# Openings of three weight units, a shorter norm chain behind the post-norms and a reordered beginning in an fp32 two-block network on one core

## The chip, the core and the metric

One core of a Trainium2 chip runs the whole program in one launch. The metric is the device time of that launch in microseconds; three runs of a kernel give its median. A profile is taken of one further execution.

## The reference

Two layers in a row on an activation of 512 positions by 1024 channels, all in fp32. Cut to what matters here:

```python
def first_block(x, ...):   # x: (1, 512, 1024)
    z = split(rmsnorm(x, norm_mix_pre) @ w_in)            # 25 column blocks of 128
    y = concat(rwkv7(z0), mlstm(z1), swa(z2), fox(z3)) @ w_out
    x = x + rmsnorm(y, norm_mix_post)
    u, g = rmsnorm(x, norm_ffn_pre) @ ffn_w_up            # 2 x 22 column blocks
    y = (u * gelu(causal_dwconv(g))) @ ffn_w_down
    return x + rmsnorm(y, norm_ffn_post)

def second_block(x, ...):
    x = x + 0.5 * swiglu(rmsnorm(x, ffn1_norm), w_gate, w_up, w_down)
    x = x + hybrid_mixer(rmsnorm(x, mix_norm), w_in, ..., w_out)
    x = x + 0.5 * swiglu(rmsnorm(x, ffn2_norm), w_gate, w_up, w_down)
    return rmsnorm(x, final_norm)
```

rmsnorm divides each position by the root of the mean square over its 1024 channels and multiplies by a gain per channel.

## The kernel before, in words

**Layout.** Activations are kept transposed: eight tiles xt[0..7] of 128 channels by 512 positions. A projection is a row of products "128x128 weight block times 128x512 tile", summed over the blocks in one PSUM bank.

**Precision by splitting.** TensorE runs in fp32r, a shorter format. Every fp32 operand is split in a head (the value rounded to fp32r) and a tail (what is left), and a block costs three products: head x head, head x tail, tail x head. For an activation tile, head(k, gain) is an ACT copy into hH[k] (with the gain as scale) and tail(k, gain, a) a DVE instruction into hL[k]. The factor of the norm, rB, is not multiplied into the tiles but into the result of the projection. So a projection behind a pre-norm can begin before rB is known; only what reads its result waits.

**Weights.** The class Stream brings them. A unit is one output column block of 128 with up to eight weight blocks of 128x128 (512 KB). SP's queue loads units in their order into two raw buffers (RAW = 2) and waits, before it loads a unit, until the unit two places before it has been split. A piece is half a unit: four blocks, 128x512. split(i) puts an ACT copy (the head) into ACT's queue and a subtraction (the tail) into DVE's; in mixer 1's projections every second subtraction goes to POOL. There are six buffers for split pieces (CUT = 6). ahead(n) (L246) issues the splits of all pieces up to n beyond the one now in use. Each split waits until its buffer has been used, which one semaphore, s_used, counts.

Every engine works through its queue in the order in which build() writes the instructions down. Inside the mixers a planner (drive_by, L400; drive, L387) chooses by estimated costs which chain writes next, with the projections as filler; elsewhere the order is that of the text.

- product / parts (L267, L314): one projection of one or three units. At the start of every piece it calls ahead(CUT - 1), thus five pieces ahead; then come four times three products.
- pair / pair_steps (L276, L285): two units side by side, block by block, so that for each tile k six products follow as soon as its head and tail are there. Used at the start of every projection behind a pre-norm, and for the first two units of mixer 1's output projection. It calls ahead(CUT - 1) at its start and its end.

**Norms.** square_in(k, ...) (L1603) has ACT square tile k and adds it to one of two sums: even k on POOL into acc, odd k on DVE into acc2. finish_norm (L1619) loads the Ln table by a small activation, sums over the channels by two fp32 products with a matrix of ones, and takes Ln and Exp (rstd_of) of the result, which gives rB. pre_norm (L1632) issues heads and tails that are not yet made, then ahead(CUT), then squares that are not yet made, and leaves finish_norm to be called later, as p.rms. A post-norm lies behind a down or output projection: project_out and ffn square each of the eight results as it comes and keep it in y[n] with its gain; add_post (L1719) then finishes the norm, multiplies y[n] by rB on DVE, adds it to xt[n] (DVE for n = 0 and 4, POOL for the others) and issues head and tail of each tile.

**Stages.** 1: mixer 1, whose output projection has a post-norm. 2: FFN 1 with a convolution, Gelu and a post-norm. 3: FFN 2 (gate, Silu, up, down) without post-norm. 4: mixer 2, no post-norm. 5: FFN 3. 6: the final norm. In an FFN the loop over f = 0..21 makes a gate and an up product each; the text behind them for that f stands ahead of the products for f + 1: multiply by rB (DVE), activation (ACT), product of both (POOL), head copy (ACT), tail (POOL). For f = 0 the products are a pair; then comes the gate product of f = 1 in bank 2 ("early"), then p.rms(). In the mixers the class Begun (L345) does this: pair, first half of a third unit, p.rms(), and the other half when its result is asked for.

**The beginning** (L1575 to L1600, L1781). ACT's queue loads two small constant arrays, pk (gains and the like) and cA (identity, ones), SP's the first weight unit, then all eight x tiles, then the second unit. All four engines wait until both constant arrays have come. Then come the splits of the first unit, heads and tails of all tiles, further splits and the squares.

## Time and profile before

| what | us |
|---|---|
| median of 3 runs | 1740.0 (1739.81 to 1741.82) |
| the profiled execution, its own time | 1741.66 |
| its span, first to last instruction | 1739.8 |
| TensorE busy | 1654.2 |
| VectorE busy | 820.3 |
| ScalarE busy | 697.7 |
| GpSimd busy | 289.2 |
| mean granted TensorE clock, as a share of full speed | 0.981 |

In the rows, PE is TensorE's products, PEld its weight loads, DVE VectorE, ACT ScalarE, POOL GpSimd, SP SyncE. "t" is any SBUF tile, "bank" a PSUM bank. A row of the timeline gives start, length, engine, line, operation, output<-input with shapes, and how many instructions were merged; in brackets, how long the engine had been idle before it and what ended that. An fp32 product (those with ones) stands as two instructions. L198 is the helper that most products come from, L304 the products of a pair, L335 the last product of a piece, L257 the ACT half and L261 the DVE or POOL half of a weight split, L158 and L165 other activations, L170, L180 and L176 DVE and POOL arithmetic.

### The profile page before, as it was taken

What the parts mean: (1) busy time and instruction counts of PE and PEld (TensorE: products, weight loads), DVE (VectorE), ACT (ScalarE), POOL (GpSimd) and SP (SyncE); (2) the same over time, 40 slices, a digit from 0 to 9 for tenths busy, and PEclk for the clock granted to TensorE, in tenths of its full rate; (3) what the DMA queues carried; (4) which work ended last, traced back from release to release, by engine and by line L of the source; (5) the groups of instructions that cost most, each with busy time, mean ns of one, the idle gap of its engine ahead of it and who ended that gap; (6) DMA issues with size and microseconds to landing.
All of it is one profiled execution on the core that took longest, in us unless ns stands there. A gap on an engine that the chain in (4) does not pass through costs nothing.

```text
span 1739.8 us, 21730 instructions
## 1 busy us (share of the span) xinstructions
PE 1654.2 (95%) x8578; PEld 1338.9 (77%) x8578; DVE 820.3 (47%) x1276; ACT 697.7 (40%) x1255; POOL 289.2 (17%) x241
## 2 busy tenths in 40 slices
PE   6999998988999999979999999999999999999995
PEld 5776776667888888858888888878887788888884
DVE  4566344355655542255444433367455444444332
ACT  5556445545433333245333332244533433333222
POOL 1221110023222210022222210000010122222001
PEclk9999998989999999999999999999999999999998
DMA  4220011121332233313222323322132232232331
GB/s 166 85 74 26 14 49 37 58 100 61 110 97 97 97 93 98 100 49 109 97 97 97 97 88 101 103 80 86 37 101 83 72 112 96 99 97 93 98 100 58
DMA packets 44133, 148.37 MB, mean 85 GB/s; under 512 B 5064, under 2 KB 6144, under 8 KB 44032
## 3 DMA queue, kind: packets, MB, share of 16 engines
q1 hardware_dynamic: 40032, 140.53, 24.9%
q10 hardware_dynamic: 4000, 6.46, 1.1%
q8 instruction: 68, 1.11, 0.3%
q14 instruction: 33, 0.27, 0.0%
HBM read 144.86 MB, written 2.10 MB: 84 GB/s over the span
## 4 chain that ended last, share of the span: by engine, by line
PE 87%; DVE 6%; ACT 5%; issue 1%; POOL 1%; DMA 0%; DVEq 0%; ACTq 0%; POOLq 0%
PE bank L198 76%; PE bank L335 6%; PE bank L304 3%; DVE t L170 3%; ACT t L158 2%; DVE t L180 2%; ACT L158 1%; PE bank L206 1%; DVE t L261 1%; ACT t L257 1%; POOL t L170 1%; DVE t L184 0%; DMA t<-in_cst 0%; DVE t L190 0%; ACT t L165 0%
## 5 line engine op out<-in xcount | busy, mean ns | idle before, releaser
L198 PE MATMUL bank<-t 128*128 128x512 f32 (+6 forms) x7578 | 1516.3, 360 | 26.8 <-DVE t L170 10.0
L198 PEld LDWEIGHTS bank<-t 128*128 128x128 f32 (+3 forms) x7578 | 1161.1, 179 | 296.8 <-issue 36.8
L261 DVE TENSOR_TENSOR t<-t 128x512 fp32r<-128x512 f32 (+1 forms) x516 | 394.3, 795 | 436.4 <-ACT t L257 428.8
L170 POOL TENSOR_TENSOR t<-t 128x512 f32<-128x512 f32 (+1 forms) x181 | 239.4, 1322 | 1210.0 <-DVE t L170 563.3
L257 ACT ACTIVATE t<-t 128x512 fp32r<-128x512 f32 (+1 forms) x540 | 310.7, 613 | 261.2 <-PE bank L335 216.9
L158 ACT ACTIVATE t<-t 128x512 f32<-128x512 f32 (+6 forms) x351 | 202.6, 605 | 357.7 <-DVE t L170 169.6
L170 DVE TENSOR_TENSOR t<-bank,t 128x512 f32<-128x512 f32 (+4 forms) x238 | 147.4, 630 | 237.2 <-PE bank L335 213.7
L335 PE MATMUL bank<-t 128*128 128x512 f32 x516 | 200.7, 389 | 0.0
L165 ACT ACTIVATE t<-t 128x512 fp32r<-128x512 f32 (+3 forms) x87 | 51.7, 606 | 250.0 <-POOL t L170 247.6
L170 DVE TENSOR_TENSOR t<-t 128x512 f32<-128x512 f32 (+7 forms) x135 | 96.6, 733 | 72.2 <-ACT t L158 62.0
L180 DVE SCALAR_TENSOR_TENSOR t<-t 128x512 f32<-128x512 f32 (+3 forms) x142 | 104.0, 748 | 39.7 <-ACT t L158 38.3
L304 PE MATMUL bank<-t 128*128 128x512 f32 x288 | 80.1, 438 | 40.8 <-DVE t L180 34.6
L335 PEld LDWEIGHTS bank<-t 128*128 128x128 f32 x516 | 96.9, 188 | 20.3
L304 PEld LDWEIGHTS bank<-t 128*128 128x128 f32 x288 | 60.3, 214 | 59.2 <-issue 34.1
L180 DVE SCALAR_TENSOR_TENSOR t<-bank,t 128x512 f32<-128x512 f32 (+5 forms) x60 | 33.1, 568 | 83.6 <-PE bank L335 60.9
L165 ACT ACTIVATE t<-bank 128x128 f32<-128x128 f32 (+5 forms) x106 | 38.2, 389 | 74.9 <-PE bank L198 47.6
L158 ACT ACT_TABLE_LOAD x50 | 64.2, 1283 | 0.9
L261 POOL TENSOR_TENSOR t<-t 128x512 fp32r<-128x512 f32 x24 | 33.6, 1401 | 148.9 <-ACT t L257 135.6
L158 ACT ACTIVATE t<-bank,t 128x512 f32<-128x512 f32 (+5 forms) x68 | 39.1, 578 | 22.1 <-PE bank L198 11.0
L158 ACT ACTIVATE t<-bank 128x512 f32<-128x512 f32 x20 | 12.0, 599 | 59.3 <-PE bank L335 38.9
L206 PE MATMUL bank<-t 128*128 128x128 f32 x196 | 30.4, 285 | 1.4 <-DVE t L170 1.3
L206 PEld LDWEIGHTS bank<-t 128*128 128x128 f32 x196 | 21.5, 142 | 7.1 <-issue 2.1
(22 smaller groups left out, 90.0 us busy)
## 6 DMA issues: line engine op xcount, KB each, us to landing
t<-in_ffn_w_up SPq DMA_DIRECT2D x88, 512.0 KB, 4.4
t<-in_w_in SPq DMA_DIRECT2D x50, 512.0 KB, 3.5
t<-in_ffn_w_down SPq DMA_DIRECT2D x48, 512.0 KB, 3.5
t<-in_ffn_w_gate SPq DMA_DIRECT2D x44, 512.0 KB, 3.4
t<-in_ffn_w_down SPq DMA_DIRECT2D x24, 384.0 KB, 3.1
t<-in_w_out SPq DMA_DIRECT2D x16, 512.0 KB, 3.5
t<-in_xt SPq DMA_DIRECT2D x8, 256.0 KB, 5.9
t<-in_xt ACTq DMA_DIRECT2D x8, 256.0 KB, 4.6
```

The costliest lines, as they stand in the source:

```text
L158: return self.av.do(lambda e: e.activation(out, in_, func, bias=bias, scale=scale, **({} if accum is None else {"accum_out": accum})), *de ...
L165: return q.do(lambda e: e.activation(out, in_, ACT.Copy), *deps, us=us)
L170: return q.do(lambda e: e.tensor_tensor(out, a, b, op), *deps, us=self.cost(out, q, True))
L180: return self.dv.do(lambda e: e.scalar_tensor_tensor(out=out, in0=a, scalar=s, in1=b, op0=op0, op1=op1), *deps, us=self.cost(out, self.dv, ...
L198: fn = lambda e: e.matmul(out, w, x, start=start, stop=stop, skip_group_check=True)
L206: fn = lambda e: e.transpose(out, in_, ident)
L257: self.p.av.put(lambda e: e.activation(hi, raw, ACT.Copy), self.s_head, 1, (self.s_load[u % RAW], 16 * (u // RAW + 1)), (self.s_used, i - ...
L261: q.put(lambda e: e.tensor_tensor(lo, raw, hi.bitcast(F), SUB), self.s_tail[i % 2], 1, (self.s_head, i + 1), before, us=0.79 if q is self. ...
L304: fn = lambda e, o=outs[u], w=w, x=x, a=(k == 0 and n == 0), z=(k == 7 and n == 2): e.matmul(o, w, x, start=a, stop=z, skip_group_check=True)
L335: pe.put(lambda e, lo=lo, x=x, stop=stop: e.matmul(out, lo, x, start=False, stop=stop, skip_group_check=True), self.s_used, 1, us=0.227)
```

## The change

- Stream has a semaphore for each of its six piece buffers in place of the one count s_used.
- pair is gone; open takes two or three units. It calls ahead(2 x units) at its start. First come, for every tile k, the products that need only the tile's head (weight head x head and weight tail x head, of all units), then, for every k, those with the tile's tail. It waits for heads (p.heads), not for tails, in its first half. It has no call of ahead at its end. pair_steps stays for mixer 1's output projection.
- FFNs open with three units (f = 0's gate and up, f = 1's gate), and p.rms() comes right behind. Begun does the same in mixer 2; in mixer 1 (late=True) it opens with two, then makes the third unit as a plain product, then calls p.rms().
- Post-norms: the Ln table is loaded ahead of the projection; sums, the two ones products over results 0 to 6, are written into product 7 (behind its first piece in an output projection, its third in a down projection); rest squares result 7 and adds it by a ones product of its own, followed by seven ones products of 384 columns whose result nobody reads, a call of ahead(CUT - 1), Ln and Exp. y[7] is made on DVE.
- add_post: all additions on DVE, all heads as they come, a call of ahead(CUT) behind tile 1, and the eight tails behind all of it. square_in takes own=True to add on DVE: for result 6 and for pre_norm's squares.
- The beginning: pk and cA have counters of their own; DVE, ACT and POOL wait for pk only, and all for cA behind the first pre_norm. x tile 0 is loaded between weight units 0 and 1, tiles 1 to 7 between units 1 and 2. acc is set to zero and three products of zeros run on TensorE. ACT's first table load comes without a wait for a transfer. The order on ACT is then split 0, head 0, splits 1 and 2, heads 1 and 2, split 3, heads 3 to 7.

The diff, cut to its core:

```diff
+        self.s_used = [sem(f"s_used{n}") for n in range(CUT)]
...
-            if u == 1:
-                others(sp)
+            if u > 0:
+                others(sp, u)
...
+    def used(self, i):
+        return (self.s_used[i % CUT], i // CUT + 1)
...
+    def open(self, outs, xh, heads, xl, *free):
+        pe, at = self.p.pe, self.at
+        part = lambda t, u, k: t[(at + 2 * u + k // 4) % CUT][:, (k % 4) * 128:(k % 4) * 128 + 128]
+        self.ahead(2 * len(outs))
+        for k in range(8):
+            for u, out in enumerate(outs):
+                i = at + 2 * u + k // 4
+                self.p.mm(out, part(self.hi, u, k), xh[k], k == 0, False, heads[k], (self.s_head, i + 1), *free)
+            for u, out in enumerate(outs):
+                self.p.mm(out, part(self.lo, u, k), xh[k], False, False, self.tail(at + 2 * u + k // 4))
+        for k in range(8):
+            for u, out in enumerate(outs):
+                fn = lambda e, o=out, w=part(self.hi, u, k), x=xl[k][0], z=k == 7: e.matmul(
+                    o, w, x, start=False, stop=z, skip_group_check=True)
+                if k % 4 == 3:
+                    pe.put(fn, self.used(at + 2 * u + k // 4)[0], 1, xl[k][1], us=0.227)
+                else:
+                    pe.quiet(fn, xl[k][1], us=0.227)
+        self.at += 2 * len(outs)
+        return [self.used(at + 2 * u + 1) for u in range(len(outs))]
...
     def product(self, W, banks, xh, xl):
         if self.rms:
-            two = [banks.next(), banks.next()]
-            m = W.pair([b.t[:, :] for b in two], xh, xl, *[b.free for b in two])
-            self.done = list(zip(two, m))
-            yield
-            self.third = W.parts(self.extra.t[:, :], 1, xh, xl, self.extra.free)
-            next(self.third)
+            three = [banks.next(), banks.next(), self.extra]
+            opened = three[:2] if self.late else three
+            m = W.open([b.t[:, :] for b in opened], xh, W.p.heads, xl, *[b.free for b in three])
+            if self.late:
+                m.append(W.product(self.extra.t[:, :], 1, xh, xl))
+            self.done = list(zip(three, m))
             self.rms()
             self.rms = None
+            yield
...
-        def load_x(sp):
-            for k in range(8):
+        def load_x(sp, u):
+            for k in {1: range(1), 2: range(1, 8)}.get(u, ()):
...
-        for q in (p.dv, p.av, p.po, p.pe):
-            q.wait(have)
+        blank = p.mset(acc[:, :], 0.0, q=p.dv)
...
+        for _ in range(3):
+            idle = p.mm(bank[6].t[:, :], acc[:, 0:128], acc[:, :], True, True, blank, last=True)
+        for q in (p.dv, p.av, p.po):
+            q.wait(named)
...
+        def sums(b):
+            p.mm(b.t[:, :], ones, acc[:, :], True, False, state["acc"], b.free)
+            state["acc_read"] = p.mm(b.t[:, :], ones, acc2[:, :], False, False, state["acc2"], last=True)
+
+        def rest(b, src, *deps):
+
+            a = p.act(sq[1][:, :], src, ACT.Square, state["sq"][1], *deps)
+            state["sq"][1] = m = p.mm(b.t[:, :], ones, sq[1][:, :], False, True, a, last=True)
+            for _ in range(7):
+                p.mm(bank[7].t[:, 0:CA], ones, cA[:, :], True, True, bank[7].free)
+            W.ahead(CUT - 1)
+            b.free, state["rB"] = rstd_of(b.t[:, :], 1.0 / 1024, eps[:, 0:1], rB[:, :], m, state.get("rB_read"))
+            return a
...
                     if f == 0:
-                        mg, mu = W.pair([bg.t[:, :], bu.t[:, :]], xh, xl, bg.free, bu.free)
-                        early = W.product(bank[2].t[:, :], 1, xh, xl, bank[2].free)
+                        three = [bg, bu, bank[2]]
+                        mg, mu, early = W.open([b.t[:, :] for b in three], xh, p.heads, xl, *[b.free for b in three])
                         p.rms()
...
+        def add_post(then, y, yt):
+
             for n in range(8):
                 a = p.tt(y[n][:, :], y[n][:, :], rB[:, :], MUL, yt[n], state["rB"])
-                xtok[n] = p.tt(xt[n][:, :], xt[n][:, :], y[n][:, :], ADD, a, xtok[n], q=p.dv if n % 4 == 0 else p.po)
-                heads.append(head(n, then))
-                if n:
-                    made[n - 1] = tail(n - 1, then, heads[n - 1])
-            made[7] = tail(7, then, heads[7])
+                xtok[n] = p.tt(xt[n][:, :], xt[n][:, :], y[n][:, :], ADD, a, xtok[n])
+                begun[n] = head(n, then)
+                if n == 1:
+                    W.ahead(CUT)
+            for n in range(8):
+                made[n] = tail(n, then, begun[n])
...
-        W.ahead(2)
+        W.ahead(1)
         if 1 in stages:
+            for k in range(8):
+                begun[k] = head(k, "norm_mix_pre")
+                if k in (0, 2):
+                    W.ahead(3 if k == 0 else 4)
+            for k in range(8):
+                made[k] = tail(k, "norm_mix_pre", begun[k])
             xh, xl = pre_norm("norm_mix_pre", bank[7])
```

## Rows read from the trace of the kernel before

**Rows 1.** The page: engines' busy time; the costliest group of PSUM reads on DVE.

```profile
PE 1654.2 (95%) x8578; PEld 1338.9 (77%) x8578; DVE 820.3 (47%) x1276; ACT 697.7 (40%) x1255; POOL 289.2 (17%) x241
...
L170 DVE TENSOR_TENSOR t<-bank,t 128x512 f32<-128x512 f32 (+4 forms) x238 | 147.4, 630 | 237.2 <-PE bank L335 213.7
```

**Rows 2.** Timeline of the boundary FFN 1 to FFN 2.

```profile
752.40 0.39 PE L335 MATMUL bank<-t 128*128 128x512 f32 x1
...
752.89 0.60 ACT L158 ACTIVATE t<-bank 128x512 f32<-128x512 f32 x1 [3.51 <-PE bank L335]
...
754.27 1.12 PE L198 MATMUL bank<-t 128*128 128x512 f32 x2 [0.61 <-DVE t L170]
...
755.12 1.28 ACT L158 ACT_TABLE_LOAD   x1
...
759.16 2.02 DVE L170 TENSOR_TENSOR t<-t 128x512 f32<-128x512 f32 x3 [3.25 <-ACT t L158]
...
763.28 4.49 PE L304 MATMUL bank<-t 128*128 128x512 f32 x12 [7.89 <-DVE t L180]
...
785.91 4.42 PE L198 MATMUL bank<-t 128*128 128x512 f32 x15
```

**Rows 3.** Stretch behind that wait: length, engines' busy time, granted clock, DMA.

```profile
763.20:766.00 2.80, 2.72 (x7) 2.19 (x8) 2.80 (x3) 0.58 (x2) 1.65 (x1) 0.50 0.00 0
```

**Rows 4.** Timeline of FFN 2: the norm's Ln, the next weight split.

```profile
787.96 0.67 ACT L158 ACTIVATE t<-bank,t 128x512 f32<-128x512 f32 x1
...
794.54 1.14 ACT L257 ACTIVATE t<-t 128x512 fp32r<-128x512 f32 x2
...
795.19 2.03 DVE L261 TENSOR_TENSOR t<-t 128x512 fp32r<-128x512 f32 x2 [3.22 <-ACT t L257]
```

**Rows 5.** The same in FFN 1, with convolution and Gelu.

```profile
407.03 0.69 ACT L158 ACTIVATE t<-bank,t 128x512 f32<-128x512 f32 x1 [0.18 <-PE bank L198]
...
416.21 2.05 DVE L261 TENSOR_TENSOR t<-t 128x512 fp32r<-128x512 f32 x2 [2.74 <-ACT t L257]
```

**Rows 6.** Timeline of the entry into mixer 2.

```profile
1130.39 11.04 PE L304 MATMUL bank<-t 128*128 128x512 f32 x48
...
1132.46 1.14 ACT L257 ACTIVATE t<-t 128x512 fp32r<-128x512 f32 x2
...
1149.48 2.78 PE L198 MATMUL bank<-t 128*128 128x512 f32 x11 [0.84 <-DVE t L170]
```

**Rows 7.** Timeline of the entry into FFN 3.

```profile
1354.13 0.39 PE L335 MATMUL bank<-t 128*128 128x512 f32 x1
...
1355.28 5.53 ACT L158 ACTIVATE t<-t 128x512 f32<-128x512 f32 x9 [3.70 <-DVE t L170]
...
1356.56 5.39 DVE L180 SCALAR_TENSOR_TENSOR t<-t 128x512 fp32r<-128x512 f32 x8
...
1357.45 12.56 PE L304 MATMUL bank<-t 128*128 128x512 f32 x48 [2.94 <-DVE t L180]
1360.72 1.14 ACT L257 ACTIVATE t<-t 128x512 fp32r<-128x512 f32 x2
...
1375.29 4.42 PE L198 MATMUL bank<-t 128*128 128x512 f32 x15
```

**Rows 8.** Timeline of the beginning.

```profile
6.07 0.25 POOL L195 MEMSET t<- 128x1 f32 x2 [5.62 <-DMA t<-in_cst]
...
8.74 4.99 ACT L158 ACTIVATE t<-t 128x512 fp32r<-128x512 f32 x8
...
15.67 12.03 PE L304 MATMUL bank<-t 128*128 128x512 f32 x45 [3.53 <-DVE t L261]
...
35.73 2.78 PE L198 MATMUL bank<-t 128*128 128x512 f32 x11 [0.83 <-DVE t L170]
```

**Rows 9.** The page's DMA issues: number, KB each, median us to landing.

```profile
t<-in_xt SPq DMA_DIRECT2D x8, 256.0 KB, 5.9
```

**Rows 10.** Timeline of the boundary mixer 1 to FFN 1, inside the opening.

```profile
393.86 5.98 PE L304 MATMUL bank<-t 128*128 128x512 f32 x18 [1.86 <-DVE t L180]
```

More of the change, by code:

```diff
@@ L1 @@
+import itertools
 import math
@@ L298, in pair_steps @@
                 ops = [(hi, xh[k]), (hi, xl(k)[0]), (lo, xh[k])]
-                signal = 1 if (k == 3 and u == 0) or (k == 7 and u == 0) else 2 if k == 7 else 0
                 pe.wait(self.tail(i), *free)
@@ L305, in pair_steps @@
                         o, w, x, start=a, stop=z, skip_group_check=True)
-                    if n >= 3 - signal:
-                        pe.put(fn, self.s_used, 1, xl(k)[1], us=0.227)
+                    if n == 2 and k % 4 == 3:
+                        pe.put(fn, self.used(i)[0], 1, us=0.227)
                     else:
@@ L533, in run @@
         pb = Banks([bank[0], bank[1]])
-        begun = Begun(p.rms, bank[3])
+        begun = Begun(p.rms, bank[3], late=True)
         end, tok, used = {}, {}, {}
@@ L1636, in pre_norm @@
             for k in range(8):
-                if made[k] is None:
-                    made[k] = tail(k, gain, head(k, gain))
+                if begun[k] is None:
+                    begun[k] = head(k, gain)
+                    made[k] = tail(k, gain, begun[k])
             W.ahead(CUT)
@@ L1699, in ffn @@
                 yt = []
+                if post:
+                    log_table()
                 for n in range(8):
                     b = bank[4 + n % 2]
-                    m = W.product(b.t[:, :], 3, [t[:, :] for t in fH],
-                                  [(fL[i][:, :], fl[i]) for i in range(22)], b.free)
-                    if post:
-                        square_in(n, b.t[:, :], m)
+                    g = W.parts(b.t[:, :], 3, [t[:, :] for t in fH],
+                                [(fL[i][:, :], fl[i]) for i in range(22)], b.free)
+                    m = ended(g, 3, (lambda: sums(bank[6])) if post and n == 7 else None)
+                    if post and n == 7:
+                        yt.append(add_last(y[n], post, b, m, bank[6]))
+                    elif post:
+                        square_in(n, b.t[:, :], m, own=n == 6)
                         b.free = t = p.act(y[n][:, :], b.t[:, :], ACT.Copy, m, scale=col(post, n))
@@ L1710, in ffn @@
                         if then:
-                            made[n] = tail(n, then, head(n, then))
+                            begun[n] = head(n, then)
+                            made[n] = tail(n, then, begun[n])
                         square_in(n, xt[n][:, :], xtok[n])
@@ L1715, in ffn, with ended, add_last @@
                 if post:
-                    add_post(then, y, yt, bank[6])
+                    add_post(then, y, yt)
                 yx.close()
-        def add_post(then, y, yt, b):
-            W.ahead(CUT)
-            finish_norm(b)
-            heads = []
+        def ended(g, n, then):
+            for i in itertools.count(1):
+                try:
+                    next(g)
+                except StopIteration as end:
+                    return end.value
+                if i == n and then:
+                    then()
+        def add_last(y, post, b, m, into):
+            a = rest(into, b.t[:, :], m)
+            b.free = t = p.ts(y[:, :], b.t[:, :], col(post, 7), None, MUL, None, a)
+            return t
+        def add_post(then, y, yt):
             for n in range(8):
                 a = p.tt(y[n][:, :], y[n][:, :], rB[:, :], MUL, yt[n], state["rB"])
-                xtok[n] = p.tt(xt[n][:, :], xt[n][:, :], y[n][:, :], ADD, a, xtok[n], q=p.dv if n % 4 == 0 else p.po)
-                heads.append(head(n, then))
-                if n:
-                    made[n - 1] = tail(n - 1, then, heads[n - 1])
-            made[7] = tail(7, then, heads[7])
+                xtok[n] = p.tt(xt[n][:, :], xt[n][:, :], y[n][:, :], ADD, a, xtok[n])
+                begun[n] = head(n, then)
+                if n == 1:
+                    W.ahead(CUT)
+            for n in range(8):
+                made[n] = tail(n, then, begun[n])
             state["rB_read"] = a
@@ L1738, in project_out @@
                 yt = []
+                if post:
+                    log_table()
                 for n in range(8):
@@ L1743, in project_out @@
                         b = bank[n % 2]
-                        m = W.product(b.t[:, :], 1, xh, xl, b.free)
-                    if post:
-                        square_in(n, b.t[:, :], m)
+                        m = ended(W.parts(b.t[:, :], 1, xh, xl, b.free), 1,
+                                  (lambda: sums(bank[2])) if post and n == 7 else None)
+                    if post and n == 7:
+                        yt.append(add_last(y[n], post, b, m, bank[2]))
+                    elif post:
+                        square_in(n, b.t[:, :], m, own=n == 6)
                         b.free = t = p.act(y[n][:, :], b.t[:, :], ACT.Copy, m, scale=col(post, n))
@@ L1756, in project_out @@
                 if post:
-                    add_post(then, y, yt, bank[2])
+                    add_post(then, y, yt)
         def done_all():
@@ L1780, in build @@
         p.eps, p.first_out = eps, None
-        W.ahead(2)
+        W.ahead(1)
         if 1 in stages:
+            for k in range(8):
[4 more added lines that the diff above has]
+                made[k] = tail(k, "norm_mix_pre", begun[k])
             xh, xl = pre_norm("norm_mix_pre", bank[7])
+            for q in (p.dv, p.av, p.po, p.pe):
+                q.wait(have)
             fence = done_all()
```

49 lines of the change are left out of this document (20 added, 29 removed).

## The prediction

> **What bounds the kernel now.** I read the page first: TensorE is busy for 1654.2 of 1739.8 us [rows 1], so a change pays only where TensorE stands still, runs slowly, or is given less to do. I then read its waits by stretch and the timeline around each. It waits at five openings: the start, the two boundaries behind a post-norm (mixer 1 to FFN 1, FFN 1 to FFN 2), the entry into mixer 2 and the one into FFN 3. In everything else a piece of four weight blocks (12 products) takes 2.72 us, end to end.
>
> At the second post-norm boundary the last product's last instruction starts at 752.40 and ends at about 752.6. Square, add, second ones product, a table load and the norm follow; the first multiplication by rB starts at 759.16 and the next opening at 763.28 [rows 2]. Twelve products then take 4.49 us instead of 2.72, at a granted clock of 0.50, which is the 1.2 GHz level, after 7.9 us without work [rows 2, 3]. The opening and the third unit are done at 785.9; the two ones products of the next norm, whose four passes of 0.43 open the row at 785.91, end at 787.6 [rows 2], and the next unit starts there without a gap, since its pieces are already split.
>
> **The queue behind the norm.** The row that decides most is on ACT. After the norm's Ln at 787.96 come Exp, Silu and the copy of f = 0; only then come weight splits, at 794.54, and the DVE half starts at 795.19 and lasts 0.69 [rows 4]: 8.0 us from Ln to a new piece that TensorE may use. With the convolution it is 407.03 to 416.21 + 0.69, thus 9.9 us [rows 5]. Today four pieces (10.9 us) are banked before the norm, because the third unit is a plain product that splits five ahead at each of its pieces. The new opening takes six pieces, all six buffers, and nothing behind it splits ahead: the next call of ahead stands in the product after f = 0's Silu or Gelu and copy (in mixer 2, in the fourth product). So TensorE must stand still from the norm's ones products to the first new piece. That is my main step; it follows from the order in which the instructions enter ACT's queue.
>
> **Post-norm boundary, FFN 1 to FFN 2** (times on the clock of the trace of before, as if nothing ahead had shifted). Two fp32 ones products, four passes of 0.43 [rows 2], move into product 7: they used to lie in a wait, now they push its end to 752.6 + 1.7 = 754.35. Square starts 0.27 later as now and lasts 0.60; its single ones product lets Ln start 1.1 later, at 756.3. The Ln table is loaded before the projection, so a load of 1.28 [rows 2] leaves this chain and hides there beside five banked pieces (if that cover were gone it would cost the 1.5 us of load and dummy). Ln 0.67, the load that remains 1.28 and Exp 0.63 give the first multiplication at 758.95: only 0.2 us earlier than 759.16. Seven fillers of 384 columns, 0.65 each, end at 760.7, in the wait, and should keep the clock up.
>
> Now DVE does it all, at 0.67 an instruction (2.02 for three [rows 2], 5.39 for eight tails [rows 7]). x0 is there at 760.3, its head (0.72) at 761.1: TensorE starts there instead of at 763.28. Behind x1 a piece is split: DVE waits for head 1 and the copy (1.4) and subtracts (0.7), so 16 instructions and 2.1 us bring x7 to 771.8 and head 7 to 772.6. TensorE's six products a block (1.36) keep pace and end at 774.0, the 24 of the second half at 779.4. Tails end at 777.2; the six square adds follow on DVE at 0.70 each (ACT 0.60 and DVE 0.69 alternate over two buffers) and end at 781.4. TensorE idles until then and ends its two ones products at 782.6: 5.0 earlier than 787.6. Ln at 782.9 (0.33 behind, as now), and 8.0 more: next unit at 790.9, **3.3 later** than now. Standing 8.3 us brings the clock down: 4.49 - 2.72 = 1.8 [rows 2]. Cost 5.1.
>
> **Mixer 1 to FFN 1.** The same, with 9.9 for 8.0: 3.3 + 1.9 + 1.8 = 7.0.
>
> **Entry of mixer 2.** No wait now: 48 products from 1130.39, the fourth unit at 1149.48 [rows 6]. The new opening's third unit is needed in block 0, but its ACT copies start at 1132.46 [rows 6], behind head and square of tile 7. TensorE, in order, stops after two products, gets the third unit's head at 1133.1 and its tail at 1134.05, and has 66 products left: 15.0, to 1149.0. Ones products to 1150.7, Ln 1151.05, Exp done at 1153.7, three evacuations at 0.63 [rows 1] that stand ahead of the split on DVE to 1155.6, the subtraction to 1156.4: 6.9 later, and 1.8 for the clock. Cost 8.7.
>
> **Entry of FFN 3.** Last product at 1354.13, ACT then runs square 7 and eight heads, 5.53 for nine; TensorE starts at 1357.45, when tail 0 is done; the splits of the third unit start at 1360.72 [rows 7]. New: head 0 is enough, so two products at 1356.6, but the third unit's first block only at 1361.3 and its tail at 1362.5; 66 products to 1377.5, and 1.7 for the clock, as the 48 show now (12.56 for 10.88 [rows 7]): 1379.2. Ones products to 1380.9, and 0.33 + 8.0: 1389.2. Now that unit starts at 1375.29 + 1.7 = 1377.0 [rows 7]. 12.2 later and 1.8 for the second cold start: cost 14.0.
>
> **The beginning.** Engines wait for constants to 6.07 and a table load follows; heads run at 8.74 at 0.62 each, products run from 15.67 (12.03 for 45, slow at first), and the fourth unit starts at 35.73 [rows 8]. New: only pk is waited for, which lies ahead of the constants, about 5.1; the table load is over. Unit 0's first split, head 0 done at 6.3; unit 1's first split needs its transfer, moved ahead of seven x transfers, so TensorE has block 0 by 8.3. x took 5.9 from issue [rows 9] and x7 is issued eighth, at about 5: it lands at about 11, head 7 at 12.3. Eight blocks at 0.91 from 8.5 with small waits end at 14.9, 16 more at 18.5, the third unit at 24.0, ones products 25.7, Ln to evacuation 3.7: fourth unit at 29.4, **6.3 earlier**. Third-unit splits (12.3) and DVE's adds, tails and splits (to 18.9) are ahead of their use. The three zero products, cold at 1.7 each, fill 1 to 6 us and cost nothing. Bounds: 2 gained if x or unit 1 comes 4 late, 9 if nothing of it waits.
>
> **At nothing:** a semaphore for each buffer (same increments); adds moved from POOL (DVE has room until the tails); the constants' later wait.
>
> **Sum:** -6.3 + 7.0 + 5.1 + 8.7 + 14.0 = +28.5. The profiled execution took 1741.66 (span 1739.8), the median of three is 1740.0; added to the median: 1768.5. The final norm shifts whole.
>
> **Two rules beside the rows.** Ln at 755.12's load is followed by another load before Exp: in this trace they never share one. The Trainium skill, ScalarE: Activation LUTs, Table sets, says that ln followed by exp needs a single load, a set holding both. The same page (What ACT_TABLE_LOAD costs) adds 1.38 us of drain to a load; here the next activation starts 0.01 to 0.02 behind the 1.28. By that drain the early load would give 1.4 more at each of two boundaries, an estimate from the page, and the sum would be 25.7.
>
> **Rivals.**
> A, the other side: the splits are ready all the same, which would need them ahead of Ln on ACT. Then each post-norm boundary gains 5.0, FFN 3 loses 3.9 (1380.9 against 1377.0), mixer 2 loses 4.9 (bank 0 is free only after Exp and one evacuation), the start gains 6.3: -7.5, 1732.5. It decides at the first weight copy behind the opening: standing before Ln on ACT. For it, ACT has idle time there; against it, the order of calls. 0.06.
> B: more cold stretches. A stop of 1.86 us in the first boundary was followed by 18 products in 5.98 us instead of 4.1 [rows 10]; four stops of 2 us in the new openings at 1.8 each: +7, 1775.5. Against it, the second boundary has stops of that length without one. 0.17.
> C: the mixers have slack, and mixer 2's 8.7 vanishes in its own chains: 1760. TensorE is full there, so 0.13.
> D: Ln and Exp get one set (the rule of the page above): 1.28 off each of five norm chains and again off two post-norm chains, -9: 1759.5. Both loads stand behind every norm now: 0.02.
> Forecast: 0.62, of which 0.04 is a half-way case (below).
>
> **Numbers.** The forecast's unknowns are the start (4 us less gain, 3 more) and four clock costs (0 to 1.8 each): 1761 to 1775. To hold 8 in 10, B and C come in and the edges: 1752 to 1780. A measurement of this kernel tells about 0.2% (3.5 us) from no change. Faster is A, 0.06, and 0.01 for splits that are late at the two entries alone; within 0.2% is 0.03, where A holds for the FFNs and not for the mixer; slower is the rest, 0.90, for which 0.03 comes off the forecast's 0.62 and D, B and C stay.
>
> **What would show it.** Right: at four openings a stop of TensorE of 8 to 10 us (5.5 in mixer 2) behind two ones products, ended by DVE's weight subtraction, with ACT's weight copies behind f = 0's copy; clock 0.50 behind each; in the two entries without post-norm a stop of 2 to 5 us after two products; fourth unit of mixer 1 at about 29; post-norm opening at about 2 us less distance. Wrong: weight copies ahead of Ln, no stop behind the ones products, or the third unit's first block split before the opening.

## The result and the profile after

The changed kernel takes 1770.97 us (median of 4 runs, 1770.06 to 1773.29); the kernel before, beside it, 1740.58 (4 runs). The ratio is 1.0176, with a 95% interval of 1.0158 to 1.0194: it is slower by 30.4 us. The profiled execution took 1770.2 us with a span of 1768.4, 28.6 more than the span before.

The page first, then the head of TensorE's list of waits (us in total, times, longest), after and, as the last line, before. Against [rows 1] TensorE is busy 17 us longer. Before, the list was led by waits of the openings for the tails of the tiles (L180), 34.6 us, and the DVE half of a weight split (L261) stood at 3.5 and 2.6 us. After, the waits for tails are down to 2.3 us, and waits for that weight split (L263) lead with 33.4.

```profile
PE 1671.5 (95%) x8616; PEld 1346.8 (76%) x8616; DVE 821.3 (46%) x1300; ACT 698.1 (39%) x1254; POOL 256.9 (15%) x218
...
PE bank L199 <- DVE t L263: 33.4, 4, 10.6
...
PE bank L304 <- DVE t L180: 34.6, 9, 10.5
```

In the changed kernel's rows L199 is the helper of products (also of an opening's first part), L323 an opening's second part, L353 the last product of a piece, L259 and L263 the halves of a weight split, L159, L166 and L171 what L158, L165 and L170 were.

The boundary FFN 1 to FFN 2, timeline of the kernel after, against [rows 2, 4]:

```profile
750.48 0.39 PE L353 MATMUL bank<-t 128*128 128x512 f32 x1
...
753.49 1.28 ACT L159 ACT_TABLE_LOAD   x1
754.78 0.63 ACT L159 ACTIVATE t<-t 128x512 f32<-128x512 f32 x1
755.44 2.75 DVE L171 TENSOR_TENSOR t<-t 128x512 f32<-128x512 f32 x4 [1.97 <-ACT t L159]
...
757.67 3.07 PE L199 MATMUL bank<-t 128*128 128x512 f32 x12 [0.41 <-ACT t L159]
...
762.33 8.46 PE L199 MATMUL bank<-t 128*128 128x512 f32 x36 [1.59 <-ACT t L159]
...
770.63 5.60 PE L323 MATMUL bank<-t 128*128 128x512 f32 x24
...
776.91 1.98 PE L199 MATMUL bank<-t 128*128 128x512 f32 x4 [0.68 <-DVE t L171]
...
778.93 0.69 ACT L159 ACTIVATE t<-bank,t 128x512 f32<-128x512 f32 x1 [0.68 <-PE bank L199]
...
785.50 2.17 ACT L259 ACTIVATE t<-t 128x512 fp32r<-128x512 f32 x4
...
786.14 3.21 DVE L263 TENSOR_TENSOR t<-t 128x512 fp32r<-128x512 f32 x4 [3.19 <-ACT t L259]
787.61 4.34 PE L199 MATMUL bank<-t 128*128 128x512 f32 x11 [8.71 <-DVE t L263]
```

The opening itself is the better one: at full clock, one stop of 1.6 us, and three units done at 776.2. The two ones products of the norm follow, and then TensorE stands 8.71 us. Ln runs at 778.93, and the first weight copies follow at 785.50, behind the work for f = 0. When the next unit starts, at 787.61, it is exactly where it stood before (787.6), though the opening had begun 5.6 us earlier (757.67 against 763.28), 3.7 of them a lead from the stages ahead. Its first 11 products take 4.34 us instead of 2.66.

The other three places, timeline of TensorE after. First the boundary mixer 1 to FFN 1, then the entry into mixer 2 [rows 6], then the entry into FFN 3 [rows 7]:

```profile
364.78 0.39 PE L353 MATMUL bank<-t 128*128 128x512 f32 x1
...
403.82 5.01 PE L199 MATMUL bank<-t 128*128 128x512 f32 x11 [10.64 <-DVE t L263]
...
1134.77 12.58 PE L199 MATMUL bank<-t 128*128 128x512 f32 x46 [2.12 <-ACT t L259]
...
1159.81 4.26 PE L199 MATMUL bank<-t 128*128 128x512 f32 x11 [5.31 <-DVE t L263]
...
1367.06 0.39 PE L353 MATMUL bank<-t 128*128 128x512 f32 x1
...
1369.51 0.73 PE L199 MATMUL bank<-t 128*128 128x512 f32 x2 [2.06 <-ACT t L159]
...
1374.32 12.45 PE L199 MATMUL bank<-t 128*128 128x512 f32 x46 [4.07 <-ACT t L259]
...
1402.63 5.06 PE L199 MATMUL bank<-t 128*128 128x512 f32 x11 [8.71 <-DVE t L263]
```

The stops of 2.12 and 4.07 us are waits for the head of the third unit's weights, wanted in the first block and split too late: two products run, then the queue stands. The beginning, after, against [rows 8]:

```profile
1.45 5.02 PE L199 MATMUL bank<-t 128*128 128x512 f32 x6 [1.45 <-DVE t L196]
...
7.91 7.64 PE L199 MATMUL bank<-t 128*128 128x512 f32 x31 [0.80 <-ACT t L259]
15.38 3.79 PE L323 MATMUL bank<-t 128*128 128x512 f32 x16
...
29.92 4.29 PE L199 MATMUL bank<-t 128*128 128x512 f32 x11 [3.60 <-DVE t L171]
```

To account for the whole, I compare the position of the same work in the two traces. A shift is the position after less the one before; the step is what the shift grew by since the row above. Before, two places are needed that the sections above do not show; timeline of TensorE, kernel before:

```profile
371.27 0.39 PE L335 MATMUL bank<-t 128*128 128x512 f32 x1
...
405.12 4.42 PE L198 MATMUL bank<-t 128*128 128x512 f32 x15
...
426.09 2.79 PE L198 MATMUL bank<-t 128*128 128x512 f32 x11 [2.60 <-DVE t L261]
```

| place | before | after | shift | forecast of the step | measured |
|---|---|---|---|---|---|
| fourth unit of mixer 1 | 35.73 | 29.92 | -5.8 | -6.3 | -5.8 |
| end of product 7 of mixer 1, without the 1.75 of moved ones products | 371.5 | 363.25 | -8.25 | 0 | -2.4 |
| unit behind the opening, FFN 1 | 406.85 | 403.82 | -3.0 | +5.2 | +5.2 |
| end of product 7 of FFN 1, the same | 752.6 | 748.95 | -3.7 | +1.8 | -0.7 |
| unit behind the opening, FFN 2 | 787.6 | 787.61 | 0.0 | +3.3 | +3.7 |
| start of the opening, mixer 2 | 1130.39 | 1132.03 | +1.6 | +1.8 | +1.6 |
| fourth unit of mixer 2 | 1149.48 | 1159.81 | +10.3 | +6.9 | +8.7 |
| start of mixer 2's last instruction | 1354.13 | 1367.06 | +12.9 | +1.8 | +2.6 |
| unit behind the opening, FFN 3 | 1377.0 | 1402.63 | +25.6 | +12.2 | +12.7 |
| final norm's first square | 1720.69 | 1749.26 | +28.6 | +1.8 | +3.0 |

The steps measured add up to 28.6, those forecast to 28.5.

### The profile page after: what moved, and what is told of

Read it like the earlier page. It is cut to its first block, busy times and chain, and to the rows that moved or that the text cites. A ratio compares the mean times of both kernels' runs of the same rounds, so it can differ in the third digit from the quotient of the medians.

```text
span 1768.4 us, 21796 instructions
## 1 busy us (share of the span) xinstructions
PE 1671.5 (95%) x8616; PEld 1346.8 (76%) x8616; DVE 821.3 (46%) x1300; ACT 698.1 (39%) x1254; POOL 256.9 (15%) x218
## 4 chain that ended last, share of the span: by engine, by line
PE 85%; DVE 7%; ACT 6%; issue 1%; DMA 1%; ACTq 0%; POOL 0%; DVEq 0%; SPq 0%; POOLq 0%
PE bank L199 76%; PE bank L353 6%; DVE t L171 3%; ACT t L159 3%; ACT L159 2%; DVE t L181 2%; PE bank L207 1%; PE bank L323 1%; DVE t L263 1%; ACT t L259 1%; PE bank L299 0%; DMA t<-in_w_in 0%; DVE t L185 0%; DVE t L191 0%; ACT t L166 0%
## 5 line engine op out<-in xcount | busy, mean ns | idle before, releaser
L199 PE MATMUL bank<-t 128*128 128x512 f32 (+7 forms) x7752 | 1575.3, 362 | 76.8 <-DVE t L263 33.4
L199 PEld LDWEIGHTS bank<-t 128*128 128x128 f32 (+4 forms) x7752 | 1200.1, 180 | 368.4 <-issue 41.5
L263 DVE TENSOR_TENSOR t<-t 128x512 fp32r<-128x512 f32 (+1 forms) x516 | 394.4, 794 | 445.1 <-ACT t L259 436.5
L259 ACT ACTIVATE t<-t 128x512 fp32r<-128x512 f32 (+1 forms) x540 | 311.2, 613 | 270.0 <-PE bank L353 222.6
L171 POOL TENSOR_TENSOR t<-t 128x512 f32<-128x512 f32 (+1 forms) x158 | 206.8, 1309 | 1247.2 <-DVE t L171 603.3
L159 ACT ACTIVATE t<-t 128x512 f32<-128x512 f32 (+6 forms) x352 | 203.3, 604 | 342.0 <-DVE t L171 180.8
L171 DVE TENSOR_TENSOR t<-bank,t 128x512 f32<-128x512 f32 (+4 forms) x238 | 147.8, 631 | 275.8 <-PE bank L353 217.9
L353 PE MATMUL bank<-t 128*128 128x512 f32 x508 | 198.1, 390 | 0.0
L166 ACT ACTIVATE t<-t 128x512 fp32r<-128x512 f32 (+3 forms) x87 | 51.7, 606 | 264.2 <-POOL t L171 261.7
L171 DVE TENSOR_TENSOR t<-t 128x512 f32<-128x512 f32 (+7 forms) x156 | 99.9, 666 | 63.3 <-ACT t L159 52.3
L181 DVE SCALAR_TENSOR_TENSOR t<-t 128x512 f32<-128x512 f32 (+3 forms) x142 | 97.6, 712 | 32.8 <-ACT t L159 31.4
L353 PEld LDWEIGHTS bank<-t 128*128 128x128 f32 x508 | 95.8, 189 | 20.1
L166 ACT ACTIVATE t<-bank 128x128 f32<-128x128 f32 (+5 forms) x106 | 38.3, 389 | 69.2 <-PE bank L199 41.8
L159 ACT ACTIVATE t<-bank,t 128x512 f32<-128x512 f32 (+5 forms) x66 | 37.9, 576 | 51.9 <-PE bank L199 40.2
L263 POOL TENSOR_TENSOR t<-t 128x512 fp32r<-128x512 f32 x24 | 33.8, 1410 | 158.3 <-ACT t L259 149.4
L159 ACT ACTIVATE t<-bank 128x512 f32<-128x512 f32 x20 | 12.0, 600 | 57.5 <-PE bank L353 40.7
L207 PEld LDWEIGHTS bank<-t 128*128 128x128 f32 x196 | 22.2, 145 | 7.1 <-DVE t L171 2.1
L323 PE MATMUL bank<-t 128*128 128x512 f32 x112 | 26.2, 389 | 0.0
L323 PEld LDWEIGHTS bank<-t 128*128 128x128 f32 x112 | 21.0, 188 | 4.4
```

The source lines that it names most:

```text
L159: return self.av.do(lambda e: e.activation(out, in_, func, bias=bias, scale=scale, **({} if accum is None else {"accum_out": accum})), *de ...
L166: return q.do(lambda e: e.activation(out, in_, ACT.Copy), *deps, us=us)
L171: return q.do(lambda e: e.tensor_tensor(out, a, b, op), *deps, us=self.cost(out, q, True))
L181: return self.dv.do(lambda e: e.scalar_tensor_tensor(out=out, in0=a, scalar=s, in1=b, op0=op0, op1=op1), *deps, us=self.cost(out, self.dv, ...
L199: fn = lambda e: e.matmul(out, w, x, start=start, stop=stop, skip_group_check=True)
L207: fn = lambda e: e.transpose(out, in_, ident)
```

## The experiments

Each is the changed kernel with one edit, unless it says otherwise; times are medians, the ratio is to the kernel before, run beside it on the same chip. The kernel before took 1738.8 us beside e1 to e4, 1739.8 beside e5 to e8 and 1740.9 beside e9 and e10, so a difference of under 2 us between these groups, or to the changed kernel, says little by itself; the rows then have to carry it.

**Splitting ahead behind the opening (e1).**

```diff
         self.at += 2 * len(outs)
+        self.ahead(CUT - 1)
         return [self.used(at + 2 * u + 1) for u in range(len(outs))]
```

> The changed kernel with one line more: the opening ends with a call that splits five pieces ahead, so that these splits stand before Ln on ScalarE. Starvation theory (TensorE stands behind the opening because no weight piece is split until the text behind the norm has run on ScalarE): the stops of 10.6, 8.7 and 8.7 us at the three FFN openings go, with the slow products behind them (2.3, 1.7, 3.0 us); the stop in mixer 2 goes down from 5.3 to some 4, the time until bank 0 is evacuated. Together about 36 us less than the changed kernel: 1735, which is below the kernel before. Rival (the clock and the norm's own length hold the openings, whatever is split): under 5 us of change, 1766 or more.

Measured: 1758.21 us, ratio 1.0109 (1.0075 to 1.0142); its four runs lie 11 us apart. Neither: 13 us less, not 36 and not under 5. The timeline of the boundary FFN 1 to FFN 2 says why:

```profile
775.44 2.17 ACT L259 ACTIVATE t<-t 128x512 fp32r<-128x512 f32 x4
775.72 4.50 PE L199 MATMUL bank<-t 128*128 128x512 f32 x15 [0.65 <-DVE t L171]
...
777.54 0.33 SPq L244 DMA_DIRECT2D t<-in_ffn_w_up  x1
...
781.24 0.63 ACT L259 ACTIVATE t<-t 128x512 fp32r<-128x512 f32 x1 [3.62 <-DMA t<-in_ffn_w_up]
...
783.29 0.67 ACT L159 ACTIVATE t<-bank,t 128x512 f32<-128x512 f32 x1
...
786.85 5.03 PE L199 MATMUL bank<-t 128*128 128x512 f32 x11 [3.68 <-DVE t L171]
```

Four copies run at once, and TensorE now goes from the ones products straight into a unit (15 products in the row at 775.72), which the changed kernel could not. But the fifth piece belongs to a unit whose transfer SP issues only at 777.54, when a raw buffer has come free; its copy waits 3.62 us on ACT, with Ln behind it. Ln runs at 783.29 instead of about 778, rB is late, and TensorE then waits 3.68 us for a bank (in mixer 2 8.4 us). The wait for weights behind the opening is gone, and a new wait, made by the added call, stands in its place.

**Four pieces instead of five (e5), and two (e7).**

```diff
+        self.ahead(4)      # e7: self.ahead(2)
```

> The changed kernel, the opening ending with a call that splits four pieces ahead instead of five. Theory: in the run with five, the fifth piece belonged to a unit whose transfer is issued only when the first pieces of this call are split, so its copy stood 3.6 to 4.6 us on ScalarE in front of Ln and put the norm off; four pieces are in the two raw buffers already. Then Ln follows the ones products at once, the two banked units (10.9 us) last until the copies behind f = 0, the stops of 8.7 to 10.6 us go with their slow products, and mixer 2 keeps one of 3.7: some 36 us less than the changed kernel, 1732 to 1737. Rival (the 13 us that five pieces gave are all there is): 1755 or more.

> As the run with four pieces, with two: one unit, 5.44 us of products, is banked ahead of the norm. Theory (a stop is the 8.3 to 10 us from Ln to a new piece, less what is banked): the FFN stops fall from 10.6, 8.7, 8.7 to about 5.2, 3.3 and 3.3, mixer 2's from 5.3 to 3.7: some 18 us less than the changed kernel, 1752 to 1755. Rival (it is the order on ScalarE alone, not the amount): as with four.

Measured: with four 1739.75 us, ratio 0.9997 (0.9987 to 1.0006); with two 1753.79 us, 1.0078 (1.0058 to 1.0098). First with four, then with two, the boundary FFN 1 to FFN 2:

```profile
771.39 4.50 PE L199 MATMUL bank<-t 128*128 128x512 f32 x15 [0.65 <-DVE t L171]
...
774.72 0.67 ACT L159 ACTIVATE t<-bank,t 128x512 f32<-128x512 f32 x1
```

```profile
773.22 4.51 PE L199 MATMUL bank<-t 128*128 128x512 f32 x15 [0.67 <-DVE t L171]
...
784.17 3.86 PE L199 MATMUL bank<-t 128*128 128x512 f32 x11 [3.50 <-DVE t L263]
```

With four, TensorE has no stop there, and none behind the ones products of FFN 3. With two, the FFN stops are 5.44, 3.50 and 3.25 us, forecast 5.2, 3.3 and 3.3: a stop is the time from the ones products to a new piece less what is banked, and each banked unit takes its 5.44 off. The dose fits the cause: TensorE starves for split weights. With four the total missed my 1732 to 1737 by some 3 us. Two terms were not in it. In FFN 1 the bank runs out before the convolution chain lets go of ACT, first for 1.07 us and then again:

```profile
415.25 3.92 PE L199 MATMUL bank<-t 128*128 128x512 f32 x11 [2.66 <-DVE t L263]
```

The second is the stop that the kernel before has at 426.09; the changed kernel lacks it, since it starves earlier. And mixer 2 kept 4.51, not 3.7: the table load for Ln stands behind the copies there, and Ln starts 1.1 us behind the ones products instead of 0.3. With two pieces that stop is 3.61.

**Openings of two units everywhere (e2).**

```diff
-                        mg, mu, early = W.open([b.t[:, :] for b in three], xh, p.heads, xl, *[b.free for b in three])
+                        mg, mu = W.open([b.t[:, :] for b in three[:2]], xh, p.heads, xl, *[b.free for b in three])
+                        early = W.product(bank[2].t[:, :], 1, xh, xl)
...
-        end, begun = {}, Begun(p.rms, bank[6])
+        end, begun = {}, Begun(p.rms, bank[6], late=True)
```

> The changed kernel with openings of two units everywhere and the third unit as a plain product behind them, as mixer 1 has it, before the norm is finished. Starvation theory: the third product splits five ahead, so four pieces are banked and the stops of 8.7 to 10.6 us go as in the run with the added call; the third unit is also no longer needed in the first block, so the stops of 2.1 and 4.1 us after two products at the two entries without post-norm go. The opening has less work per tile in the post-norm boundaries, so it stutters by some 0.4 us a tile; about 1733 to 1740. Rival (three units or two makes no difference, the loss lies in additions and tails moved to VectorE): 1766 or more.

Measured: 1736.76 us, ratio 0.9984 (0.9973 to 0.9994). As expected: no stop at the FFNs behind the ones products, none after two products at the entries. This undoes just the third unit of the opening and takes 34 us off: the changed kernel's whole loss lies there, and what remains of the change stands 2 us below the kernel before. Mixer 2 keeps a stop of 3.6 us and FFN 1 one of 2.65.

**Third unit's splits ahead of the heads (e6)**, with four pieces as in e5.

```diff
+            W.ahead(CUT)
             for k in range(8):
                 if begun[k] is None:
                     begun[k] = head(k, gain)
                     made[k] = tail(k, gain, begun[k])
-            W.ahead(CUT)
```

> As the run with four pieces, and in the pre-norm the third unit's splits are issued ahead of the heads. Theory: at the entry into FFN 3 TensorE no longer stops 4.1 us behind two products; it starts 1.1 us later, since head 0 stands behind two copies, and gains 3 to 3.5 us in all: 1729 to 1734. Elsewhere nothing changes, since the call finds its pieces split. Rival: the heads, now later, hold the opening instead, no gain.

Measured: 1735.96 us, ratio 0.9974 (0.9964 to 0.9984), 3.8 less than e5, a little over the gain expected; the total is 2 above the range given, since e5 had been expected lower than it came. Timeline at the entry of FFN 3: one start, no stop behind two products, though the clock is low for longer (48 products in 14.00). Not all of the 3.8 need come from there: in this trace the 46 products behind mixer 2's stop of 2.12 us took 11.00 us, where they took 12.62 in e5's behind the same stop.

```profile
1348.47 1.13 ACT L259 ACTIVATE t<-t 128x512 fp32r<-128x512 f32 x2
...
1350.27 14.00 PE L199 MATMUL bank<-t 128*128 128x512 f32 x48 [3.10 <-ACT t L159]
```

**The old beginning (e3).**

```diff
-            for k in {1: range(1), 2: range(1, 8)}.get(u, ()):
+            for k in {1: range(8)}.get(u, ()):
...
+        for q in (p.dv, p.av, p.po, p.pe):
+            q.wait(named, have)
...
-        W.ahead(1)
+        W.ahead(2)
```

(with the products of zeros and the order of heads and splits undone too).

> The changed kernel with the old beginning: x transfers together behind the first weight unit, all engines waiting for both constant arrays, two splits first, heads and tails in turn, no products of zeros. Theory: the fourth unit of mixer 1 starts some 6 us later than in the changed kernel, at about 36, and the 4 us that mixer 1 gains beyond that come from slow stretches of TensorE's clock that may or may not come back: 1777 to 1781. Rival (the beginning's gain is lost again in mixer 1's chains): 1771.

Measured: 1782.05 us, 11.1 more than the changed kernel and 1 above the range given; ratio 1.025 (1.0229 to 1.0271). TensorE's rows:

```profile
15.93 9.25 PE L199 MATMUL bank<-t 128*128 128x512 f32 x29 [0.18 <-DVE t L263]
...
39.55 2.90 PE L199 MATMUL bank<-t 128*128 128x512 f32 x6 [3.59 <-DVE t L171]
```

The fourth unit starts at 39.55, 9.6 later than at 29.92, and not at 36. So the new beginning is worth 9.6 us, and other parts of the change cost 3.8 in the same place (39.55 against 35.73 [rows 8]). Of these, 2.7 are the norm: mixer 1 now makes its third unit whole before it, and nothing lies beside Ln and Exp; the stop there is 3.6 us where it was 0.8. The other 1.1 lie in the opening, behind which the third unit starts at 28.64 against 27.54: the 29 products at 15.93 took 9.25 us, where 6.6 is the full-speed time.

**No products of zeros (e10).**

```diff
-        for _ in range(3):
-            idle = p.mm(bank[6].t[:, :], acc[:, 0:128], acc[:, :], True, True, blank, last=True)
+        idle = blank
```

> The changed kernel without the three products of zeros at its beginning. Theory that they bring the clock up before the first weights come: without them the first 32 products run at the slow level for a while, as before the change, and the fourth unit of mixer 1 starts 1 to 2 us later than 29.9; the time 1771 to 1774. Rival: the waits between the first products let the clock fall either way, no difference in that start.

Measured: 1775.58 us (2 runs), ratio 1.0201 (1.0183 to 1.022). TensorE's rows and, below them, the stretch 9 to 12 us (length, busy us with number of instructions by engine, granted clock, DMA share, GB/s), here and in the changed kernel:

```profile
7.90 9.68 PE L199 MATMUL bank<-t 128*128 128x512 f32 x31 [0.52 <-ACT t L259]
...
31.96 2.46 PE L199 MATMUL bank<-t 128*128 128x512 f32 x8 [3.59 <-DVE t L171]
...
9.00:12.00 3.00, 3.00 (x9) 2.32 (x8) 2.07 (x4) 3.00 (x6) 0.00 (x0) 1.00 1.06 412
```

```profile
9.00:12.00 3.00, 3.00 (x15) 2.43 (x14) 2.18 (x4) 3.00 (x6) 0.00 (x0) 1.00 1.06 414
```

31 products take 9.68 us instead of 7.64, and the fourth unit starts 2.0 later. With the three idle products they took 7.59 to 7.64 us in eight of nine traces, and 9.22 in the ninth (e9): the idle products mostly do what they are for, not always. The median lies 2.6 us beyond the 2.0, with two runs only and an interval that overlaps the changed kernel's; the trace has 4.2 us of excess in mixer 1, in a stretch that differs by as much between kernels that share it (see the last section).

**No idle products behind the post-norms (e4).**

```diff
-            for _ in range(7):
+            for _ in range(0):
```

> The changed kernel without the seven products of ones behind each post-norm, whose results nobody reads. Theory that they keep the clock up: both post-norm openings begin at the slow level and lose 1.8 us each, but their stutter behind tile 1 takes up part of it, so 1 to 3.5 us more than the changed kernel, 1772 to 1774.5. Rival: no difference, since the opening is paced by VectorE at 1.33 us a tile.

Measured: 1771.63 us, ratio 1.0188 (1.0162 to 1.0214): no difference that these runs can tell, and under the 1 us that was the least expected. The trace has one:

```profile
374.01 13.99 PE L199 MATMUL bank<-t 128*128 128x512 f32 x48 [4.92 <-ACT t L159]
...
376.00:380.00 4.00, 4.00 (x11) 3.13 (x10) 3.90 (x7) 1.44 (x2) 0.00 (x0) 0.50 0.40 131
```

After 4.92 us without work the opening starts at a granted clock of 0.50, but its first part takes 13.83 us (374.01 to 387.84) instead of 13.03, as slow products only fill the stop behind tile 1 and the room that VectorE's pace leaves. Seven idle products save 0.8 us at each of two boundaries.

**The two ones products behind product 7 (e8).**

```diff
-                    m = ended(g, 3, (lambda: sums(bank[6])) if post and n == 7 else None)
+                    m = ended(g, 3, None)
...
+            sums(into)
             a = rest(into, b.t[:, :], m)
```

(and in project_out the same).

> The changed kernel with the two ones products over results 0 to 6 moved from the middle of product 7 to behind it. Theory of my sum: inside the product they push its end by 1.75 us, behind it they lie in the wait for the square and lengthen the chain by some 0.85, so about 0.9 us less at each of two boundaries: 1768 to 1770.5. Rival (moving them in shortens the chain as meant): 1 us or more longer at each, 1773 or more.

Measured: 1768.82 us, ratio 1.0165 (1.015 to 1.018), 2.2 less than the changed kernel, as expected; but the intervals of the two ratios overlap, so it is the rows that show it. Last product to opening:

```profile
749.00 7.25 PE L199 MATMUL bank<-t 128*128 128x512 f32 x20
...
756.66 3.05 PE L199 MATMUL bank<-t 128*128 128x512 f32 x12 [0.41 <-ACT t L159]
```

From 749.0 to 756.66 it takes 7.66 us; in the changed kernel 6.97 from the end of product 7 and 1.75 inside it, 8.72. Moving the sums into the product shortens the chain by 0.7 and lengthens the queue by 1.75: 1.06 us lost at each of two boundaries.

**What comes together (e9):** e2 and e8, and in the mixers the norm after half of the third unit.

```diff
-                m.append(W.product(self.extra.t[:, :], 1, xh, xl))
+                self.third = W.parts(self.extra.t[:, :], 1, xh, xl)
+                next(self.third)
...
+        if self.third:
+            g, self.third = self.third, None
+            m = yield from g
+            return self.extra, m
```

> Openings of two units everywhere with the third unit as a plain product; in the two mixers the norm is finished after the first half of that third unit, as in the kernel before, and the two ones products over results 0 to 6 stand behind product 7. Theory: against the run with openings of two units alone (1736.8) the stops of 3.6 us before the fourth unit of both mixers shrink to 0.8, as in the kernel before, since 2.72 us of products lie beside Ln and Exp, and some slow products behind the mixer 2 stop go; 0.9 each at two boundaries for the ones products: 1726 to 1731, faster than both kernels. Rival: the mixers' chains give it back, 1735 or more.

Measured: **1725.33 us, ratio 0.9912 (0.9898 to 0.9925)**, just below the range that I gave, and faster than both kernels: 15.6 us under the kernel before, 46 under the changed one. TensorE in mixer 1's opening, then the fourth units of mixer 1 and mixer 2:

```profile
8.37 9.22 PE L199 MATMUL bank<-t 128*128 128x512 f32 x31 [1.28 <-ACT t L259]
...
29.25 2.78 PE L199 MATMUL bank<-t 128*128 128x512 f32 x11 [0.79 <-DVE t L171]
...
1135.61 2.75 PE L199 MATMUL bank<-t 128*128 128x512 f32 x11 [0.84 <-DVE t L171]
```

The stops are 0.79 and 0.84 us, where e2 has 3.59 and 3.61. In mixer 1 the fourth unit is just 0.7 us earlier than in the changed kernel, as the opening ran slowly in this trace. From the opening's second half to that unit it takes 11.82 us, 2.7 less than the changed kernel's 14.54, which is the length of the half unit that now lies beside Ln and Exp. Against e2, the rows give 2.8 in each mixer for the stops, 2.3 for the 11 products behind mixer 2's (5.03 there), and 1.06 at each boundary, 10 of the 11 us between the medians.

## Why the prediction was right

The forecast was 1768.5, the median is 1770.97; against its own base, the difference of the spans, +28.5 was forecast and +28.6 came. That closeness is partly luck, as the table shows.

- **The main step held.** No weight piece is split between the opening and the text behind the norm. Stops of 10.64, 8.71, 8.71 and 5.31 us ended by DVE's subtraction; forecast 8 to 10 and 5.5. e7 shows the law by its dose, e2 and e5 that the loss goes with it. Rival A (1732.5) had the size of what lies behind it about right: with the splits ahead of Ln the kernel takes 1739.75, and the convolution chain and mixer 2 account for part of the 7 between.
- **The post-norm boundaries** came out at +5.2 and +3.7 for 5.2 and 3.3. The chain's 0.2, the stop behind tile 1, the squares at the end: each within 0.3 us of its row (opening 6.97 behind product 7's end, forecast 6.8).
- **The entries** held in kind (two products, then a stop of 2.12 and 4.07), +8.7 for 6.9 and +12.7 for 12.2. The 1.8 missing at mixer 2 is clock: 46 products behind a stop of 2.12 us took 12.58 us where 10.4, 46 times 0.227, is the full-speed time. I had charged none, and had that only in rival B.
- **The clock's price was mis-sized.** I took 1.8 us for each stop. The 11 products behind took 2.35, 1.7, 1.6 and 2.4 us more than 2.66, and some slow ones follow; with mixer 2's opening that is about 4 us more than the sum. Rival B was half true.
- **The beginning's net held, its parts did not.** I had -6.3, it was -5.8. The -6.3 itself rests on a slip: eight blocks at 0.91 us from 8.5 end at 15.8, not at 14.9, and the same working then gives -5.4 and a total of +29.4. e3 shows -9.6 for the new beginning, +2.7 for the third unit made whole in mixer 1 ahead of the norm, and +1.1 in the opening. My working had both the earlier start and the 3.7 us from the ones products to the fourth unit, but never named the latter as a cost of its own, and so I missed that it could be undone.
- **What I had at nothing and was not:** mixer 1 shifted by a further -2.4 although it lost 1.6 behind the fourth unit, and FFN 1 by -3.0 against the clock's cost. The second is mostly the stop of 2.60 us at 426.09 in the kernel before, which a kernel that starved earlier does not have; the prediction had said that everything outside the five openings runs end to end, and had missed it. The first is no larger than what chance does in single traces, see below. Together they hid the clock's excess.
- **The range's working does not add up as written.** The unknowns listed (the start by 3 down and 4 up, four clock costs of 0 to 1.8 that the sum has at full already) give 1758 to 1772.5, not 1761 to 1775. And two of the four clock costs came out above the 1.8 that was their upper end.
- **Ln, Exp and the loads:** the load left the post-norm chain as the sum had it, and the one between Ln and Exp stayed (753.49), the next activation 0.01 us behind it. Neither the shared set nor the drain that the Trainium skill, ScalarE: Activation LUTs, has under Table sets and What ACT_TABLE_LOAD costs shows in these traces.

Left open: how the few us between e2, e5 and e6 divide between their stops and the chance of the clock. The two edits of e9 were not run apart in the mixers, so their shares are read from rows. The additions moved to DVE and the early table load were never undone by themselves; only e2, which keeps them, shows that they do not carry the loss.

## What to carry to other kernels

When an opening takes every buffer at once, ask where the next refill stands in each engine's queue, not only whether a buffer is free: here a better opening lost 8.7 us behind it because the refill stood behind a norm and an activation. Refill ahead of the long wait, but only with what has already arrived: one piece too many put a transfer's wait in front of that same norm. And count work moved into a busy queue at its full length: 1.75 us of sums took 1.06 us more inside the product than behind it, where they lay in a wait.

## What the runs showed of the hardware

**The same short stop may or may not slow the products behind it.** Mixer 1 holds the same work in both kernels behind its fourth unit. One stretch of 75 small and large products behind a stop of 1.2 us, first before, then after, TensorE's timeline and the granted clock in it:

```profile
207.53 13.73 PE L198 MATMUL bank<-t 64*64 64x64 f32 x75 [1.16 <-ACT t L165]
...
214.00:217.50 3.50, 3.50 (x15) 2.81 (x15) 0.25 (x1) 0.55 (x2) 0.00 (x0) 0.50 0.00 0
```

```profile
203.47 10.61 PE L199 MATMUL bank<-t 64*64 64x64 f32 x75 [1.20 <-ACT t L166]
...
210.60:214.20 3.60, 3.60 (x20) 3.03 (x19) 0.42 (x1) 1.22 (x3) 1.08 (x1) 1.00 0.00 0
```

The same products take 3.1 us more where the clock fell to 0.50, the 1.2 GHz level. From the fourth unit to the long wait near 300 us the time was 266.3 us in the kernel before, 263.3 in the changed kernel, and 261.8 (e2) to 267.5 (e10) in the nine experiments that have the changed kernel's mixer 1, all but e9. Chance of that size lies in every single trace here, so the table's second step can't be told from it. Mixer 2 shows the same behind a stop of 2.12 us: its 46 products took 12.40 to 12.63 us in eight traces and 11.00 in the ninth (e6).

**The recorded clock is not to be trusted at the start.** In e10 9 products ran from 9 to 12 us where the changed kernel ran 15, and both rows give a granted clock of 1.00. The Trainium skill, TensorE: Matmul & The Clock Gate, warns under Seeing it yourself that such clock events were seen to be unreliable; here the count of products in the stretch shows it.
